# Encoder trunk, one core: the second layer's small vectors turned during the up products, not in the opening

## The reference

```
mod = silu(c) @ ada_w[l] + ada_b[l]              # 6 x 1024: sh1, sc1, g1, sh2, sc2, g2
h = rmsnorm(x, norm_mix_g[l]) * (1 + sc1) + sh1
x = x + g1 * mixer(h)                            # l = 0: gated recurrence and neighbourhood attention
                                                 # l = 1: dilated attention and pooling
h = rmsnorm(x, norm_ffn_g[l]) * (1 + sc2) + sh2
gate, val = split(h @ w_up[l])                   # 2 x 2816 columns
gate = conv_b[l] + sum_j shifted(gate, j) * conv_w[l][j]      # 3 taps along the tokens
x = x + g2 * ((silu(gate) * val) @ w_down[l])
```

## Time and profile before

| what | us |
|---|---|
| runs before | 769.1 (median of 3), 761.99, 772.46 |
| profiled execution, its own time | 767.33 |
| its span, first to last instruction | 765.7 |
| TensorE busy | 729.7 (95%) |
| VectorE (DVE) busy | 568.3 (74%) |
| ScalarE (ACT) busy | 421.8 (55%) |
| GpSimd (POOL) busy | 66.1 (9%) |

### The profile page before, as it was taken

One profiled execution on the slowest core, in us unless ns is written; L12 is line 12 of the kernel. 1 busy time (PEld: TensorE's weight loads), 2 busy tenths in 40 slices (PEclk: granted clock), 3 DMA queues, 4 the chain that ended last, 5 costly groups with the idle time before them and its releaser, 6 DMA issues.

```text
span 765.7 us, 16582 instructions
## 1 busy us (share of the span) xinstructions
PE 729.7 (95%) x6577; PEld 702.3 (92%) x6577; DVE 568.3 (74%) x790; ACT 421.8 (55%) x698; POOL 66.1 (9%) x94
## 2 busy tenths in 40 slices
PE   3889999989999999999999999999999999999997
PEld 3877789978899999999999998998899999999997
DVE  4876886896789999876667779777477778776343
ACT  4363589713765656553365465566566556565332
POOL 2011110002000101001010009000003000000001
PEclk9989999999999999999999999999999999999999
DMA  9999778813478999768749987752239777755501
GB/s 316 370 316 329 266 246 271 305 37 111 111 200 266 287 290 289 269 234 284 249 160 312 339 290 236 243 198 88 59 108 296 225 228 228 229 191 195 188 31 56
DMA packets 163443, 171.27 MB, mean 224 GB/s; under 512 B 5453, under 2 KB 142358, under 8 KB 163392
## 3 DMA queue, kind: packets, MB, share of 16 engines
q1 hardware_dynamic: 155584, 143.13, 59.8%
q0 software_dynamic: 7808, 27.43, 9.9%
HBM read 169.49 MB, written 1.05 MB: 223 GB/s over the span
## 4 chain that ended last, share of the span: by engine, by line
PE 71%; DVE 13%; DMA 5%; ACT 4%; SPq 3%; issue 2%; DVEq 0%; ACTq 0%
PE acc L1563 48%; PE big L1563 14%; DVE w_lo L1048 4%; DMA ada_raw<-in_ada_w 4%; SPq L380 2%; DVE qk L366 2%; DMA w_raw<-in_even_w_in 2%; ACT w_hi L613 1%; DVE work L1118 1%; PE big L1679 1%; DVE h_lo L1125 1%; PE big L2061 1%; SPq L395 1%; DVE mod_acc L1061 1%; DVE mod_acc L1402 1%
## 5 line engine op out<-in xcount | busy, mean ns | idle before, releaser
L1563 PE MATMUL acc<-h_hi,w_hi 128*128 128x256 f32 x1136 | 321.9, 283 | 11.6 <-DVE h_lo L1176 4.6
L1048 DVE TENSOR_TENSOR w_lo<-w_raw,w_hi 128x1024 fp32r<-128x1024 f32 x214 | 261.3, 1244 | 80.9 <-ACT w_hi L613 80.8
L1563 PE MATMUL acc<-h_lo,w_hi 128*128 128x256 f32 x1136 | 317.6, 280 | 0.0
L1563 PE MATMUL acc<-h_hi,w_lo 128*128 128x256 f32 x1136 | 317.4, 279 | 0.0
L613 ACT ACTIVATE w_hi<-w_raw 128x1024 fp32r<-128x1024 f32 x214 | 218.8, 1050 | 93.6 <-PE acc L1563 73.7
L1563 PEld LDWEIGHTS acc<-h_hi,w_hi 128*128 128x128 f32 x1136 | 215.1, 189 | 15.3 <-issue 9.3
L1563 PEld LDWEIGHTS acc<-h_hi,w_lo 128*128 128x128 f32 x1136 | 216.3, 190 | 0.0
L1563 PEld LDWEIGHTS acc<-h_lo,w_hi 128*128 128x128 f32 x1136 | 215.3, 190 | 0.1
L1563 PE MATMUL big<-hid_hi,w_hi 128*128 (+1 forms) x308 | 86.1, 279 | 0.0
L1563 PE MATMUL big<-hid_lo,w_hi 128*128 (+1 forms) x308 | 85.7, 278 | 0.0
L1563 PE MATMUL big<-hid_hi,w_lo 128*128 (+1 forms) x308 | 85.7, 278 | 0.0
(11 more groups left out here) (278 smaller groups left out, 982.9 us busy)
## 6 DMA issues: line engine op xcount, KB each, us to landing
w_raw<-in_ffn_w_up SPq DMA_DIRECT2D x88, 512.0 KB, 5.1
ada_raw<-in_ada_w POOLq DMA_DIRECT2D x52, 512.0 KB, 5.5
w_raw<-in_ffn_w_down SPq DMA_DIRECT2D x44, 512.0 KB, 4.3
w_raw<-in_odd_w_in SPq DMA_DIRECT2D x40, 512.0 KB, 5.7
w_raw<-in_even_w_in SPq DMA_DIRECT2D x32, 512.0 KB, 9.7
ada_raw<-in_ada_w SPq DMA_DIRECT2D x24, 512.0 KB, 4.9
ada_first<-in_ada_w SPq DMA_DIRECT2D x12, 512.0 KB, 10.0
w_raw<-in_even_w_out SPq DMA_DIRECT2D x8, 512.0 KB, 4.2
```

The lines of the kernel that those rows point to most:

```text
L1048: dve.tensor_tensor(w_lo[:, half_slot(n), part], w_raw[:, n % RAW, part], w_hi[:, half_slot(n), part].bitcast(F32), ALU.subtract).then_inc ...
L1563: ins = pe.matmul(dst, lhsT, rhs, start=start and n == 0, stop=stop and n == 2, skip_group_check=True)
```

## The change

The columns of `vecs` are ordered anew: 169 early ones, with the first layer's vectors, and 160 late ones, with the second layer's and `final_norm_g`. The opening loads 161 rows by eight DMAs of POOL and turns them by three transposes; ACT copies 169 columns. The 160 late rows are loaded by twelve DMAs of POOL behind the first layer's tile DMAs into two tiles of 80 rows (`rows_late`). Ahead of the fourth unit (u = 3) of each up product TensorE turns one of the two tiles, into a PSUM bank of its own. ACT copies it behind that unit's `hid_hi` in three pieces (`keep_late`) and waits for them; its units 0 to 3 are written out for that, ahead of a loop of four times four. The first tile holds `ada_b`, the norms and the first four units' taps of the second layer; the second tile holds `final_norm_g` and the other units' taps. POOL waits for all six pieces ahead of `fin`. The diff, cut to its core:

```diff
-V_C, V_ADAB = 0, 8
-V_NMIX, V_NFFN, V_FIN, V_PSC, V_LB, V_HG, V_CB = 104, 120, 136, 144, 148, 152, 153
-V_CW = 197
-V_ALL = V_CW + 2 * 3 * FT
+V_PSC, V_LB, V_HG, V_C, V_ADAB, V_EARLY, V_FIN = 16, 20, 24, 113, 121, 169, 233
+V_NMIX, V_NFFN, V_CB, V_CW = (0, 217), (8, 225), (25, 241), (47, 263)
+LATE_ROWS, LATE_AT, LATE_U = 80, 3, 4
+V_ALL = V_CW[1] + 3 * FT
...
+        rows_late = sb("rows_late", [P, 2, P])
...
@@ gpsimd
-            pool.dma_start(rows_a[8:104, :], ada_b.rearrange("l (k p) -> (l k) p", p=P)).then_inc(s_rows, 16)
...
-            for l in (0, 1):
-                pool.dma_start(rows_c[:, l, :], ffn_conv_w[l].rearrange("j (k p) -> (j k) p", p=P)).then_inc(s_rows, 16)
+            by_rows = lambda a: a.rearrange("(k p) -> k p", p=P)
+            pool.dma_start(rows_a[8:56, :], by_rows(ada_b[0])).then_inc(s_rows, 16)
...
+            pool.dma_start(rows_c[:], ffn_conv_w[0].rearrange("j (k p) -> (j k) p", p=P)).then_inc(s_rows, 16)
             first_tiles(0, ADA1_POOL)
+            def late_rows(part, row, vectors):
+                pool.dma_start(rows_late[row:row + vectors.shape[0], part, :], vectors).then_inc(s_late, 16)
+            late_rows(0, 0, by_rows(ada_b[1]))
+            late_rows(0, 48, by_rows(norm_mix_g[1]))
+            late_rows(0, 56, by_rows(norm_ffn_g[1]))
+            late_rows(1, 0, by_rows(final_norm_g))
+            late_rows(0, 64, by_rows(ffn_conv_b[1])[0:LATE_U])
+            late_rows(1, 8, by_rows(ffn_conv_b[1])[LATE_U:FT])
+            for tap in range(3):
+                late_rows(0, 68 + tap * LATE_U, by_rows(ffn_conv_w[1, tap])[0:LATE_U])
+                late_rows(1, 26 + tap * (FT - LATE_U), by_rows(ffn_conv_w[1, tap])[LATE_U:FT])
             pool.wait_ge(mod_gathered, 2)
...
             pool.wait_ge(h_lo_ready, NORM_AT[3] + KT)
+            pool.wait_ge(late_kept, 6)
             for k in range(KT):
                 ins = pool.tensor_scalar(fin[:, k, :], ident, vecs[:, V_FIN + k:V_FIN + k + 1], None, ALU.mult)
@@ scalar
+            def keep_late(part):
+                act.wait_ge(late_turned, part + 1)
+                taps = vecs[:, V_CW[1]:V_CW[1] + 3 * FT].rearrange("p (j u) -> p j u", j=3)
+                if part == 0:
+                    pieces = ((vecs[:, V_EARLY:V_FIN], 0, 64), (vecs[:, V_CB[1]:V_CB[1] + LATE_U], 64, 68),
+                              (taps[:, :, 0:LATE_U], 68, 80))
+                else:
+                    pieces = ((vecs[:, V_FIN:V_FIN + KT], 0, 8), (vecs[:, V_CB[1] + LATE_U:V_CB[1] + FT], 8, 26),
+                              (taps[:, :, LATE_U:FT], 26, 80))
+                for to, first, last in pieces:
+                    turned_rows = aux[:, 1, first:last]
...
+                    nc.scalar.activation(to, turned_rows, ACT.Copy).then_inc(late_kept, 1)
+                act.wait_ge(late_kept, 3 * part + 3)
...
-            nc.scalar.activation(vecs[:, 0:V_ALL], aux[:, 0, 0:V_ALL], ACT.Copy).then_inc(vecs_ready, 1)
+            nc.scalar.activation(vecs[:, 0:V_EARLY], aux[:, 0, 0:V_EARLY], ACT.Copy).then_inc(vecs_ready, 1)
...
-                up_step(0, first_up)
-                stream(act, first_up + 1, N_UP - 1, 4, up_step)
+                for u in range(LATE_AT + 1):
+                    up_step(0, first_up + u)
+                keep_late(l)
+                stream(act, first_up + LATE_AT + 1, N_UP - LATE_AT - 1, 4, up_step)
@@ tensor
-            pe.wait_ge(s_rows, 16 * 10)
-            pe.transpose(aux[:, 0, 0:104], rows_a[:], ident[0:104, 0:104])
-            pe.transpose(aux[:, 0, 104:197], rows_b[:], ident[0:93, 0:93])
-            for l in (0, 1):
-                at0 = V_CW + l * 3 * FT
-                ins = pe.transpose(aux[:, 0, at0:at0 + 3 * FT], rows_c[:, l, :], ident[0:3 * FT, 0:3 * FT])
+            pe.wait_ge(s_rows, 16 * 8)
+            pe.transpose(aux[:, 0, 0:47], rows_b[:], ident[0:47, 0:47])
+            pe.transpose(aux[:, 0, 47:113], rows_c[:], ident[0:3 * FT, 0:3 * FT])
+            ins = pe.transpose(aux[:, 0, 113:V_EARLY], rows_a[:], ident[0:56, 0:56])
             ins.then_inc(rows_turned, 1)
...
-                units(first_up, first_up + 1, N_UP - 1, feature_major, hid_ready, l * FT, fresh=3, h_from=NORM_AT[idx])
+                units(first_up, first_up + 1, LATE_AT - 1, feature_major, hid_ready, l * FT, fresh=3, h_from=NORM_AT[idx])
+                split_ready(0, 2, first_up + LATE_AT)
+                pe.wait_ge(hid_ready, l * FT + LATE_AT - 1)
+                pe.wait_ge(s_late, 16 * 12)
+                pe.transpose(aux[:, 1, 0:LATE_ROWS], rows_late[0:LATE_ROWS, l, :],
+                             ident[0:LATE_ROWS, 0:LATE_ROWS]).then_inc(late_turned, 1)
+                units(first_up, first_up + LATE_AT, N_UP - LATE_AT, feature_major, hid_ready, l * FT, fresh=3)
```

More of the change, by code:

```diff
@@ L218, in encoder @@
         x_tok = at("x_tok", [P, TT, D], F32, arena + 40 * K)
-        rows_a = at("rows_a", [104, P], F32, arena + 48 * K)
-        rows_b = at("rows_b", [93, P], F32, arena + 49 * K)
-        rows_c = at("rows_c", [3 * FT, 2, P], F32, arena + 50 * K)
+        rows_a = at("rows_a", [56, P], F32, arena + 48 * K)
+        rows_b = at("rows_b", [47, P], F32, arena + 49 * K)
+        rows_c = at("rows_c", [3 * FT, P], F32, arena + 50 * K)
         RPB_RUN = 5 * (2 * NA_KC - 1) + GRID_W
@@ L317, in encoder @@
         rstd_kept = sem("rstd_kept")
+        s_late, late_turned, late_kept = sem("s_late"), sem("late_turned"), sem("late_kept")
         strips_summed, strips_kept = sem("strips_summed"), sem("strips_kept")
@@ L537, in link @@
                 pool.wait_ge(pool_step, done[0])
-            pool.dma_start(rows_a[8:104, :], ada_b.rearrange("l (k p) -> (l k) p", p=P)).then_inc(s_rows, 16)
[L540 to L546, removed]
-            for l in (0, 1):
-                pool.dma_start(rows_c[:, l, :], ffn_conv_w[l].rearrange("j (k p) -> (j k) p", p=P)).then_inc(s_rows, 16)
+            by_rows = lambda a: a.rearrange("(k p) -> k p", p=P)
+            pool.dma_start(rows_a[8:56, :], by_rows(ada_b[0])).then_inc(s_rows, 16)
+            pool.dma_start(rows_b[0:8, :], by_rows(norm_mix_g[0])).then_inc(s_rows, 16)
+            pool.dma_start(rows_b[8:16, :], by_rows(norm_ffn_g[0])).then_inc(s_rows, 16)
+            pool.dma_start(rows_b[16:20, :], by_rows(pool_scale[0])).then_inc(s_rows, 16)
+            pool.dma_start(rows_b[20:24, :], by_rows(hgrn_lb_logits[0])).then_inc(s_rows, 16)
+            pool.dma_start(rows_b[24:25, :], hgrn_norm_g).then_inc(s_rows, 16)
+            pool.dma_start(rows_b[25:47, :], by_rows(ffn_conv_b[0])).then_inc(s_rows, 16)
+            pool.dma_start(rows_c[:], ffn_conv_w[0].rearrange("j (k p) -> (j k) p", p=P)).then_inc(s_rows, 16)
             def first_tiles(first, last):
@@ L636, in keep_rstd @@
                 nc.scalar.activation(rstd[:], aux[:, 0, T:2 * T], ACT.Copy).then_inc(rstd_kept, 1)
+            def keep_late(part):
[9 more added lines that the diff above has]
+                    turned_rows = aux[:, 1, first:last]
+                    if len(to.shape) == 3:
+                        turned_rows = turned_rows.rearrange("p (j u) -> p j u", j=3)
+                    nc.scalar.activation(to, turned_rows, ACT.Copy).then_inc(late_kept, 1)
+                act.wait_ge(late_kept, 3 * part + 3)
             def whole_shifts(idx, n, scale):
@@ L871, in up_step @@
                     nc.scalar.activation(conv[:, a, :], big[:, 0, 0:T] if whole else acc[:, a, 0:T], ACT.Identity,
-                                         bias=vecs[:, bass.ds(i * 4 + (V_CB + l * FT + u), 1)],
-                                         scale=vecs[:, bass.ds(i * 4 + (V_CW + l * 3 * FT + FT + u), 1)]
+                                         bias=vecs[:, bass.ds(i * 4 + (V_CB[l] + u), 1)],
+                                         scale=vecs[:, bass.ds(i * 4 + (V_CW[l] + FT + u), 1)]
                                          ).then_inc(conv_mid, 1)
@@ L1162, in take_scale @@
                 dve.scalar_tensor_tensor(out=gain[:, 0, part], in0=mods[:, 0, rows], scalar=1.0,
-                                         in1=vecs[:, V_NMIX + part.start:V_NMIX + part.stop], op0=ALU.add,
+                                         in1=vecs[:, V_NMIX[0] + part.start:V_NMIX[0] + part.stop], op0=ALU.add,
                                          op1=ALU.mult).then_inc(done, 1)
@@ L1327, in _ @@
             take_mods(1, 0, 16, 24, acc[:, 1])
-            make_gain(1, 0, 32, V_NFFN)
+            make_gain(1, 0, 32, V_NFFN[0])
             split_lo(0, EO + 1)
@@ L1415, in step @@
                         nu = i * 4 + (l * FT + u)
-                        tap = lambda j: vecs[:, bass.ds(i * 4 + (V_CW + l * 3 * FT + j * FT + u), 1)]
+                        tap = lambda j: vecs[:, bass.ds(i * 4 + (V_CW[l] + j * FT + u), 1)]
                         whole = isinstance(i, int) and u == 0
@@ L1460, in ffn @@
                     take_mods(2, 0, 40, 24, aux[:, 1])
-                    make_gain(2, 1, 8, V_NMIX + KT)
```

(3 more changed lines are left out.)

## The result

The changed kernel took 771.86 us (median of 6 runs, 768.45 to 776.43), the kernel before, run beside it on the same chip, 765.99 (6 runs, 760.61 to 772.46). The ratio is 1.0117, with a 95% interval of [1.0077, 1.0156]: 9 us slower, 6 to 12. Ratios leave out disturbed executions, so they are not the quotients of the medians. The forecast, 769.9 us, lies 2 us under the time of after, but on a base of 768.2; the step from before to after was forecast as 1.7 us and is 9. That the time itself lies so near is luck: the base was 2.2 us too high, and the step several times too small.

The account below looks back on a forecast made before the run. TensorE's multiplies were taken to bound the up products, loads the opening. -0.3 (opening) + 0.4 (two transposes) + 1.6 (late tile) = +1.7 us on 768.2 gave 769.9 us, range 762 to 776.

Parts of the forecast that it names:

- Opening: Opening's loads: fewer rows by POOL's DMAs bring the weights 0.3 us earlier; bounds 0 and 1.1 us.
- Late DMAs: Twelve DMA issues on POOL between the issue at 121.69 and the wait ending at 179.87: cost 0, bound 0.3 us.
- Transposes: One transpose ahead of each up product's fourth unit: 0.2 us each, 0.4 us for two; bounds 0.15 and 0.8.
- Copies on ACT: Three copies behind the fourth unit's hid_hi, about 0.5 us in a row, hidden in ACT's idle time; bounds 0 and 0.3 us.
- The late tile, 1.6 us: Second up product: POOL's later fin delays tile 24, DVE stands 3.4 us, TensorE loses 1.6 us; bounds 1.0 and 6.0.
- a wait of over 7 us ahead of tile 24's step: Sign of being wrong: DVE's wait at L1400, forecast as 3.4 us, lasting under 1 us or over 7.
- `fin` runs 4.64 us to the next issue: Step on POOL in the second up product: fin takes 4.64 us, so tile 24 is issued at 600.4.
- I take 4.7: Step: tile 24 lands 4.7 us after its issue, at 605.1; earlier tiles of this queue took 4.1 to 9.1.
- the rival built on a landing of 3.2 us: Tile 24 lands in time, in 3.2 us or less; TensorE within 0.1 us of its place; 768.4 us, chance 0.12.
- Clock: Rival: after TensorE's idle at the eighth unit the granted clock falls, costing 2.5 us more; 772.4 us, chance 0.08.
- here full work stands right before the idle: Argument against the clock falling at the eighth unit: in the opening, where it fell to 0.50, no full work preceded.
- the late landing's: Rival: tile 24 takes 9.1 us to land, the loss is 6.0 us instead of 1.6; 774.3 us, chance 0.15.

Follow-up runs that it names:

- Experiment 3: Only the opening's part of the change, late vectors left out as columns of ones, against the kernel before: 766.91 us, ratio 1.0003 [0.9964, 1.0042].
- experiment 7: The change with six of fin's eight products issued ahead of tiles 24 and 25, two behind: 768.46 us against 768.22 for the kernel before.
- experiment 2: The change with POOL issuing tiles 24 and 25 ahead of its wait for ACT's copies and fin, against the kernel before: 766.57 us, ratio 1.0039.
- experiment 6: The kernel before with fin waiting for hid_hi of the second up product's fifth unit, one later than in the change: 769.33 us against 768.22.
- experiments 10 and 11: The kernel before with an unused rows_late buffer allocated, and with one more opening transpose: 766.29 and 762.96 us against 765.00, ratios 1.0002 and 0.9991.
- experiment 1: The same changed kernel, unedited, measured again against the kernel before: 771.99 us against 764.76, ratio 1.0129 [1.0080, 1.0179].

## Why the prediction was right in its mechanism and wrong in its size

*Opening.* Forecast -0.3 us, bounds 0 and 1.1. Experiment 3: no difference that shows, and its interval of 3 us either way is too wide for 0.3; first convolution of the first up product: 0.7 to 1.0 us earlier by the means, within the spread. Nothing contradicts the bounds; the 0.3 us is not confirmed.

*Late DMAs.* Forecast 0, behind L516's last early issue and ahead of POOL's long wait. They stand at 119.95 to 126.04, with 52.06 us of idle behind. Right.

*Transposes.* Forecast 0.2 us each. The row of 0.29 us at 589.07, and units longer by 0.21 to 0.29 us than in kernels without them: 0.5 us for both against 0.4.

*Copies on ACT.* Forecast hidden. The three take 0.34 us with 0.18 of wait for their end, and ACT waits for TensorE again behind them:

```profile
598.77 0.34 ACT L671 ACTIVATE vecs<-aux 128x8 f32<-128x8 f32 x3
599.29 0.20 ACT L702 ACTIVATE table_sink<-consts 128x1 f32<-128x1 f32 x1 [0.18 <-ACT vecs L671]
601.12 0.57 ACT L907 ACTIVATE conv<-acc,vecs 128x256 f32<-128x256 f32 x1 [1.62 <-PE acc L1601]
```

Right; the earlier trace rows had 1.90 us of wait there.

*The late tile, 1.6 us: the term that failed, with the right mechanism.* To compare, I count from the fourth unit's first multiply, 585.43 in the forecast and 589.36 in after:

```
                                        forecast   measured
fin starts                               10.4        9.9
tile 24 is issued                        15.0       16.8
tile 24 is used                          19.7       23.6
DVE would have been ready for it         16.3       16.5
DVE stands                                3.4        7.07
DVE, first tap to second w_lo's end       3.67       3.66
TensorE's gap                             1.6        5.14
the clock's part                          0          2.2
```

The prediction named a wait of over 7 us ahead of tile 24's step as a sign of being wrong: it was 7.07 us in after and 6.96 in its repetition. Two steps were mis-sized. "`fin` runs 4.64 us to the next issue" took a duration from a place where DVE did other work and moved it to one where DVE subtracts 1024 columns for `w_lo`: the same eight instructions took 6.9 us. The extra 2.27 us lie in three products of 1.00, 1.33 and 1.74 us where the others take 0.60. The Trainium skill says in "SBUF — State Buffer", section "Who interferes with whom", that a VectorE instruction with two inputs in SBUF contends with a GpSimd instruction that reads SBUF, and that whichever is issued second waits out the first. The trace agrees: the last product lost 1.14 us beside a subtraction of 1.21 that had started 0.2 us ahead of it. The first one lost 0.41 us beside a `hid_lo` of 0.42; there its own record starts first, so the order is not shown. The prediction should have weighed it. And "I take 4.7" for the landing rested on the DMA engines' idleness between 600.5 and 602.6. The later issue, at 606.20, fell together with two w_raw halves of SP instead, and the landing took 6.63 us:

```profile
605.69 1.00 SPq L424 DMA_DIRECT2D w_raw<-in_ffn_w_up  x2
```

Each of the two errors is 1.9 us or more; DVE's slack of 1.8 us was already spent, so all of it went into TensorE's gap. The slack itself held well: DVE's stand less TensorE's gap is 1.9 us in after and in its repetition, and 1.6 to 1.7 in the four other kernels with a gap.

The bounds had room for the landing (to 9.1 us) and none for `fin`. The Trainium skill's page "DMA: Bandwidth & Descriptors", section "Anatomy of one DMA — SWDGE (gpsimd) path", makes it an estimate of 3.2 us for 512 KB. The kernels here that issue tiles 24 and 25 late had 4.2 to 7.3 us for them, so the rival built on a landing of 3.2 us has fallen.

*Clock.* It had a chance of 0.08, because "here full work stands right before the idle". That argument fails: full work stood before the 5.14 us as well. For the 1.6 us that I had forecast, experiment 7 suggests that the clock would have stayed up: it did behind 1.31 us. The clock's rival and the late landing's were no alternatives to each other: one makes the gap that sets off the other. Their prices (+2.5 for the clock, 6.0 for the loss without it) come near the measured 2.2 and 5.1, the second by luck: it supposed a landing of 9.1 us where 6.63 was measured, and knew nothing of the longer `fin`.

*The time.* 771.86 us lies in the range of 762 to 776 because the runs' own spread made that range wide, not because the sum was good. Taken over the base, the sum of the measured parts (0 to -1.0, 0.5 and 7.3 us) is some 7 to 8 us, inside the measured 6 to 12.

No version of the change was shown to beat the kernel before: without the late tile it is at 1.0039 [1.0000, 1.0078].

## What to carry to other kernels

A wait added to one engine is paid by whatever stands behind it in that engine's queue. Here the vectors were in time, and the two DMA issues behind them were not; issue what others wait for first, then wait. A duration is a property of an instruction and of its neighbours: when one moves, look at what the other engines and queues do at its new place. And when a gap on TensorE is forecast, price the granted clock with it, by whether rows of similar gaps show it to fall.

## What the hardware showed that I had not expected

*POOL beside DVE.* A product of 128x128 fp32 on POOL takes 0.60 us; beside DVE's `hid_lo` 0.69 to 1.15, and beside one of DVE's 128x1024 subtractions for `w_lo` 0.96 to 1.76. The longest, 2.19 us in experiment 2, met a subtraction, `hid_lo` and tile 24's own step, one after another. The subtraction took up to 1.40 us instead of 1.23. Eight products took 4.68 us in before, 5.21 with DVE mostly idle, 6.94 to 7.49 with DVE at work. The delay is not spread over the eight: it comes whole, in the one to three products that meet such an instruction. An experiment with DVE's second input elsewhere than in SBUF was not tried.

*Landing of a 512 KB tile.* Issued by POOL 0.5 to 1.1 us behind the first of two w_raw halves, tile 24 took 6.5 to 6.7 us (five kernels). Issued 1.2 us ahead of them it took 4.2 (six products ahead), 2 us behind them 4.8 (four ahead), and with none near it 4.35 (experiment 6). No run moved the w_raw halves by themselves.

*What a stop adds through the clock.* In the five kernels with a stop of 5.0 to 7.1 us, the two units around it lost 1.6 to 2.3 us more than the stop itself, without growing with its length.

*Two paces of TensorE at one granted clock.* Windows in the middle of each up product, first before, then after:

```profile
230.00:320.00 90.00, 90.00 (x797) 90.00 (x796) 83.39 (x115) 54.06 (x86) 8.45 (x16) 1.00 0.92 284
630.00:690.00 60.00, 60.00 (x512) 60.00 (x511) 47.54 (x68) 35.74 (x57) 1.59 (x3) 1.00 0.71 215
```
```profile
230.00:320.00 90.00, 90.00 (x766) 90.00 (x765) 81.35 (x111) 53.85 (x87) 8.32 (x16) 1.00 0.91 279
630.00:690.00 60.00, 60.00 (x532) 60.00 (x531) 49.79 (x72) 36.71 (x57) 2.11 (x4) 1.00 0.76 227
```

TensorE is busy throughout at 1.00 in all four, yet the multiplies of L1563 and L1601 are either 113.4 or 117.8 ns apart. The pace holds through a stretch and changes only where TensorE has stopped; over the 958 multiplies of the first up product's undisturbed part it is 4.2 us. In the first product all seven profiled kernels with the new opening ran at 117.8 ns, and all six with the old one at 113.4. In the second, kernels of both kinds ran at either. So about 4 us between two profiled executions, up or down, may be this and nothing of the change: after lost 4.2 us by it in the first product and gained 3 us back behind the gap in the second. A seven-to-six split may point at the opening, but experiment 3 has the slow pace there and a ratio of 1.0003, and experiments 10 and 11 rule out two causes. The times alone show steps of this size within one kernel: of the 26 runs of before beside experiment 1, 12 lie from 759.2 to 761.9 us, 12 from 764.7 to 767.4, two above 771, and none between. Whether these are the paces is not shown, since only a profiled execution has a trace. What sets the pace stays open.
